# A two-block transformer forward pass on one Trainium2 core: expert weights streamed in pairs of 16 KB rows through ten buffers, with ten units of the fixed expert first

## The reference

```python
def moe_swiglu(u, w_router, w_gate, w_up, w_down):
    logits = (t @ w_router).astype(F32)
    top_vals, top_idx = lax.top_k(logits, TOP_K)
    ...
    for e in range(N_EXPERTS):
        y = swiglu(t, w_gate[e], w_up[e], w_down[e]).astype(F32)
        out = out + gates[:, e:e + 1] * y
```

## Time and profile before

| | us |
|---|---|
| median of 3 runs | 1735.1 (1733.96 to 1736.97) |
| the profiled execution, its own time | 1736.92 |
| its span | 1735.1 |
| mean granted TensorE clock | 0.989 |
| TensorE busy | 1633.8 (94%) |
| VectorE busy | 1000.9 (58%) |
| ScalarE busy | 847.7 (49%) |
| DMA read from HBM | 485.24 MB, 282 GB/s over the span |

### The profile page before, as it was taken

The page is one execution under the profiler, slowest core; times in us unless marked ns, Lnnn a source line. Parts: engine busy times, 40 slices in busy tenths (PEclk is TensorE's granted clock), DMA queues, the critical chain, the costliest instruction groups (busy, mean ns, idle before and its releaser), DMA issues.

```text
span 1735.1 us, 22075 instructions
## 1 busy us (share of the span) xinstructions
PE 1633.8 (94%) x8466; PEld 1178.0 (68%) x8466; DVE 1000.9 (58%) x1347; ACT 847.7 (49%) x1109; POOL 24.2 (1%) x31
## 2 busy tenths in 40 slices
PE   9989899999999999999989999887999989999886
PEld 7877788888878888898766666334665656566432
DVE  7986699847767885577576463004463644645000
ACT  6976677646656553566355353004453544444100
POOL 0000000000000000000000000000000000000000
PEclk9999999999999999999999999999999999999998
DMA  9332355544324555443259999999999999999996
GB/s 377 134 138 97 122 183 183 195 168 170 122 73 176 188 194 194 149 167 134 110 240 422 421 420 419 407 422 414 422 422 421 421 404 422 421 420 422 405 421 272
DMA packets 68940, 490.66 MB, mean 283 GB/s; under 512 B 7776, under 2 KB 8160, under 8 KB 9952
## 3 DMA queue, kind: packets, MB, share of 16 engines
q1 hardware_dynamic: 67248, 484.48, 69.9%
q0 software_dynamic: 1584, 4.72, 1.2%
HBM read 485.24 MB, written 3.93 MB: 282 GB/s over the span
## 4 chain that ended last, share of the span: by engine, by line
PE 68%; DMA 18%; DVE 7%; ACT 5%; issue 1%; POOL 0%; SPq 0%; ACTq 0%; DVEq 0%; POOLq 0%
DMA raw<-in_units 12%; PE ps L495 10%; PE ps L631 9%; PE ps L1408 9%; PE ps L504 8%; PE ps L497 8%; DMA x<-in_units 5%; PE ps L634 5%; PE ps L1425 4%; DVE wl L3533 2%; PE ps L515 2%; DVE wl L2518 1%; ACT wh L2312 1%; PE ps L935 1%; PE ps L936 1%
## 5 line engine op out<-in xcount | busy, mean ns | idle before, releaser
L2518 DVE TENSOR_TENSOR wl<-raw,wh 128x2048 fp32r<-128x2048 f32 x124 | 283.1, 2287 | 81.8 <-ACT wh L1677 81.5
L3533 DVE TENSOR_TENSOR wl<-raw,wh 128x2048 fp32r<-128x2048 f32 x97 | 221.8, 2290 | 171.7 <-ACT wh L2312 171.6
L1677 ACT ACTIVATE wh<-raw 128x2048 fp32r<-128x2048 f32 x125 | 238.4, 1913 | 70.1 <-PE ps L504 69.0
L2312 ACT ACTIVATE wh<-raw 128x2048 fp32r<-128x2048 f32 x96 | 183.7, 1917 | 122.1 <-PE ps L504 121.5
L1408 PE MATMUL ps<-raw,hT_f 128*64 128x512 f32 x424 | 198.0, 612 | 35.0 <-DMA raw<-in_units 33.3
L495 PE MATMUL ps<-wh,hT_both 128*128 128x512 f32 (+2 forms) x568 | 224.4, 397 | 6.3 <-DVE hT_both L2828 1.6
L497 PE MATMUL ps<-wh,hT_both 128*128 128x512 f32 (+2 forms) x568 | 216.8, 384 | 0.0
L1409 PE MATMUL ps<-raw,hT_f 128*64 128x512 f32 x416 | 196.6, 619 | 0.0
L631 PE MATMUL ps<-hT_both,wh 128*128 128x512 f32 x704 | 179.0, 396 | 2.7 <-DVE hT_both L2576 2.6
L1408 PEld LDWEIGHTS ps<-raw,hT_f 128*64 128x64 f32 x424 | 55.7, 140 | 149.4 <-issue 147.8
L504 PE MATMUL ps<-wl,hT_both 128*128 128x512 f32 (+2 forms) x568 | 151.1, 383 | 0.0
(11 more groups left out here) (502 smaller groups left out, 2612.4 us busy)
## 6 DMA issues: line engine op xcount, KB each, us to landing
raw<-in_units SPq DMA_DIRECT2D x384, 1024.0 KB, 14.0
xn<-in_units SPq DMA_DIRECT2D x37, 1024.0 KB, 15.0
x<-in_units SPq DMA_DIRECT2D x37, 1024.0 KB, 15.1
x<-in_x SPq DMA_DIRECT2D x2, 512.0 KB, 5.7
work<-in_lru_w SPq DMA_DIRECT2D x1, 1024.0 KB, 15.9
xn<-in_mem SPq DMA_DIRECT2D x1, 1024.0 KB, 15.4
out<-x POOLq DMA_DIRECT2D x2, 512.0 KB, 3.1
consts<-in_consts POOLq DMA_DIRECT2D x1, 768.0 KB, 4.7
```

The costliest lines, as they stand in the source:

```text
L1677: A(wh[:, n % SPLIT, :], raw[:, n % RAW, :], ACT.Copy).then_inc(sem("hi_made"), 1)
L2312: A(wh[:, (N_FIXED + j) % SPLIT, :], raw_at(n), ACT.Copy).then_inc(sem("hi_made"), 1)
L2518: V.tensor_tensor(wl[:, n % SPLIT, :], raw[:, n % RAW, :], wh[:, n % SPLIT, :].bitcast(F32), ALU.subtract).then_inc(sem("lo_made"), 1)
L3533: V.tensor_tensor(wl[:, s, :], raw_at(STREAM_AT[g, 0, EXPERT_ORDER[j]]), wh[:, s, :].bitcast(F32), ALU.subtract).then_inc(sem("lo_made"), 1)
```

## The change

- The expert weights lie in HBM in pairs: the two halves of a gate, up or down are put side by side, so that one row of a pair has 16 KB. One DMA loads a pair (2 MB) into two neighbouring buffers, and one semaphore tells of both.
- The ring has ten buffers: `raw` gets an eighth, which is also `xn`; the other two are `x` and the last 2048 columns of `work`, side by side. `esg` and the routing tables move out of `work` into `consts`.
- The load of a pair waits until both units of the pair that it overwrites, ten places back, are free.
- The narrow units are loaded in the order gate 0, gate 1, up 0, up 1, where it was gate 0, up 0, gate 1, up 1. TensorE uses them as before.
- `AHEAD = 4` takes the place of `SPLIT` (3) in the stream: four wide units come ahead of the loop. So units 8 to 13 (in the first group 10 to 13) are loaded ahead of the narrow units of chunk 1, and 14 to 19 ahead of those of chunk 2. `SPLIT` is still 3 for `wh` and `wl`.
- In the first group ten units of the fixed expert come first. Seven are loaded as before, the eighth after the last transposes of the stage ahead (`hgrn_oT_ps`), and the ninth and tenth as a pair into the buffers of units 0 and 1, once those are split. All three go ahead of the wait for `ordered`.
- The branch for overfull experts, which is not taken with these inputs, is rewritten for the new layout in HBM.

```diff
-RING = RAW + 2
+RING = RAW + 3
...
-STREAM = [(0, 0, _u) for _u in EXPERT_ORDER[:SPLIT]]
+NARROW_IN_PAIRS = []
+for _c in range(ECH + 1):
+    if _c < ECH:
+        NARROW_IN_PAIRS += [("gate", _c, 0), ("gate", _c, 1), ("up", _c, 0), ("up", _c, 1)]
+    if _c > 0:
+        NARROW_IN_PAIRS += [("down", _c - 1, 0), ("down", _c - 1, 1)]
+AHEAD = 4
+STREAM = [(0, 0, _u) for _u in EXPERT_ORDER[:AHEAD]]
 for _g, (_w, _) in enumerate(GROUPS):
     for _c in range(ECH):
-        _at = 6 * _c + (1 if _c == 0 else -2) + (2 if _c == 0 else 3)
-        _wide = EXPERT_ORDER[_at:_at + (4 if _c == 0 else 6)] if _w is not None else []
-        STREAM += [(_g, 0, _u) for _u in _wide] + [(_g, 1, _u) for _u in NARROW_ORDER if _u[1] == _c - (_u[0] == "down")]
+        _more = 2 if _g == 0 else 0
+        _at = AHEAD if _c == 0 else 2 + 6 * _c + (_more if _c == 1 else 0)
+        _wide = EXPERT_ORDER[_at:_at + (4 + _more if _c == 0 else 6 - _more if _c == 1 else 6)] if _w is not None else []
+        STREAM += [(_g, 0, _u) for _u in _wide] + [(_g, 1, _u) for _u in NARROW_IN_PAIRS if _u[1] == _c - (_u[0] == "down")]
     if _g + 1 < NG and GROUPS[_g + 1][0] is not None:
-        STREAM += [(_g + 1, 0, _u) for _u in EXPERT_ORDER[:SPLIT]]
+        STREAM += [(_g + 1, 0, _u) for _u in EXPERT_ORDER[:AHEAD]]
     STREAM += [(_g, 1, ("down", ECH - 1, _h)) for _h in range(2)]
...
-    x = sb("x", [TT, D])
...
-    xn = sb("xn", [TT, D])
     work_at = nc.sbuf_base
-    work = sb("work", [WORK])
+    work_and_x = sb("work_and_x", [WORK + UNIT])
+    work = work_and_x[:, 0:WORK]
+    x = work_and_x[:, WORK:].rearrange("p (t d) -> p t d", t=TT)
...
+    raw = sb("raw", [RAW + 1, UNIT])
+    xn = raw[:, RAW, :].rearrange("p (t d) -> p t d", t=TT)
...
-    esg = area(11264, HALF)
+    esg = consts[:, dist_at:dist_at + HALF]
...
+    def place_in_ring(n):
+
+        i = n - N_FIXED
+        return i if i <= RAW else (0, 8, 2, 4, 6)[(i - RAW - 1) // 2 % 5] + i % 2
...
+    FIRST_PAIR = N_FIXED + RAW + 1
+
+    def signal_of(n):
+
+        return slot_of(n if n < FIRST_PAIR else n - (n - N_FIXED) % 2)
...
-    spare = [xn_flat, x[:].rearrange("p t d -> p (t d)")]
-
     def raw_at(n):
 
-        return raw[:, slot_of(n), :] if slot_of(n) < RAW else spare[slot_of(n) - RAW]
+        m = place_in_ring(n)
+        at = WORK - UNIT + UNIT * (m - RAW - 1)
+        return raw[:, m, :] if m <= RAW else work_and_x[:, at:at + UNIT]
+
+    def raw_pair(n):
+
+        m = place_in_ring(n)
+        return raw[:, m:m + 2, :].rearrange("p a n -> p (a n)") if m < RAW else work_and_x[:, WORK - UNIT:]
...
+        pairs_d = units_d.rearrange("(a b) p n -> a (b p n)", b=2).rearrange("a (p m) -> a p m", p=P)
+
+        def of_pair(pair, half):
+            return pairs_d[pair][:, half * UNIT:(half + 1) * UNIT]
...
+        for n in range(N_FIXED, N_FIXED + RAW):
+            sp_.wait_ge(sem("lo_made"), n - RAW + 1)
+            load(None, n, of_pair(n // 2, n % 2))
...
+        sp_.wait_ge(*reached("hgrn_oT_ps", 4))
+        n = N_FIXED + RAW
+        sp_.dma_start(raw_at(n), of_pair(n // 2, n % 2)).then_inc(raw_loaded[signal_of(n)], 16)
+        for overwritten in (N_FIXED, N_FIXED + 1):
+            freed(overwritten)
+        sp_.dma_start(raw_pair(FIRST_PAIR), pairs_d[FIRST_PAIR // 2]).then_inc(raw_loaded[signal_of(FIRST_PAIR)], 16)
         sp_.wait_ge(sem("ordered"), 1)
-        at = [nc.sync.value_load(order[0:1, s:s + 1], min_val=N_FIXED, max_val=N_FIXED + (NE - 1) * E_UNITS) for s in range(NE)]
-        for n in range(N_FIXED + RAW, N_UNITS):
+        at = [nc.sync.value_load(order[0:1, s:s + 1], min_val=N_FIXED // 2, max_val=(N_FIXED + (NE - 1) * E_UNITS) // 2) for s in range(NE)]
+        for n in range(FIRST_PAIR + 2, N_UNITS, 2):
             g, narrow, what = STREAM[n - N_FIXED]
-            if n - RING >= N_FIXED:
-                freed(n - RING)
-            elif n == N_FIXED + RAW:
-                sp_.wait_ge(*reached("hgrn_oT_ps", 4))
+            assert what[2] == 0 and STREAM[n + 1 - N_FIXED] == (g, narrow, (what[0], what[1], 1))
+            if n > FIRST_PAIR + 2:
+                for overwritten in (n - RING, n - RING + 1):
+                    freed(overwritten)
             else:
                 sp_.wait_ge(sem("out_written"), 16 * TT)
                 sp_.wait_ge(sem("tokens_left"), 2)
-            sp_.dma_start(raw_at(n), units_d[at[GROUPS[g][narrow]] + UNIT_OF[what]]).then_inc(raw_loaded[slot_of(n)], 16)
+            sp_.dma_start(raw_pair(n), pairs_d[at[GROUPS[g][narrow]] + UNIT_OF[what] // 2]).then_inc(raw_loaded[signal_of(n)], 16)
 
...
-            put(N_FIXED + e * E_UNITS + j, k_tiles(w))
+            beside = [k_tiles(w)] if half == 0 else beside + [k_tiles(w)]
+            if half == 1:
+                put_pair(N_FIXED + e * E_UNITS + j - 1, beside)
```

More of the change, by code:

```diff
@@ L181, in area, with routing_area @@
         return v
+    def routing_area(at, *shape):
+        v = consts[:, CONST["dist"] + at:CONST["dist"] + at + int(np.prod(shape))]
+        return v if len(shape) == 1 else v.rearrange("p (a b) -> p a b", a=shape[0])
     def const(name, n, at=0):
@@ L409, in build @@
     logitsT = work[0:NE, 12992:12992 + S]
[L410 to L417, removed]
+    rcmp = [routing_area(HALF + 128 * i, TT * NE * NE) for i in range(2)]
+    slots = routing_area(768, NE + OVER + 2, TT)
+    places = routing_area(820, NE + OVER, TT)
+    gates = routing_area(868, NE + OVER, TT)
+    by_turn = routing_area(916, NE, NE)
+    place_of, gate_of = routing_area(980, TT, NE), routing_area(996, TT, NE)
+    load_of, turn_of, in_turn_of = routing_area(1012, NE), routing_area(1020, NE), routing_area(1028, NE)
     order = sb("order", [NE], I32)
@@ L451, in fixed_loads @@
         return len(range(slot, N_FIXED, RAW)) if slot < RAW else 1
+    FIRST_PAIR = N_FIXED + RAW + 1
+    def signal_of(n):
+        return slot_of(n if n < FIRST_PAIR else n - (n - N_FIXED) % 2)
     def raw_of(n):
-        return raw_loaded[slot_of(n)], 16 * (fixed_loads(slot_of(n)) + (n - N_FIXED) // RING + 1)
+        slot = signal_of(n)
+        loads = [m for m in range(N_FIXED, n + 1) if signal_of(m) == slot and (m < FIRST_PAIR or (m - N_FIXED) % 2 == 0)]
+        return raw_loaded[slot], 16 * (fixed_loads(slot) + len(loads))
     def raw_again(j):
         slot = (N_FIXED + j) % RAW
-        before = sum(slot_of(n) == slot for n in range(N_FIXED, N_UNITS))
+        before = len([n for n in range(N_FIXED, N_UNITS)
+                      if signal_of(n) == slot and (n < FIRST_PAIR or (n - N_FIXED) % 2 == 0)])
         return raw_loaded[slot], 16 * (fixed_loads(slot) + before + j // RAW + 1)
-    spare = [xn_flat, x[:].rearrange("p t d -> p (t d)")]
     def raw_at(n):
-        return raw[:, slot_of(n), :] if slot_of(n) < RAW else spare[slot_of(n) - RAW]
+        m = place_in_ring(n)
[4 more added lines that the diff above has]
+        return raw[:, m:m + 2, :].rearrange("p a n -> p (a n)") if m < RAW else work_and_x[:, WORK - UNIT:]
     def counted(ins, name, by=1):
@@ L1617, in _ @@
                 sp_.dma_start(rows[:], rows_d.partition_broadcast(P)).then_inc(sem("rows_loaded"), 16)
-        assert (N_FIXED + RAW - head) % RAW == 0 and all(u[:2] == (0, 0) for u in STREAM[:RAW])
-        with nc.sync.Fori(0, (N_FIXED + RAW - head) // RAW) as g:
+        pairs_d = units_d.rearrange("(a b) p n -> a (b p n)", b=2).rearrange("a (p m) -> a p m", p=P)
+        def of_pair(pair, half):
+            return pairs_d[pair][:, half * UNIT:(half + 1) * UNIT]
+        assert (N_FIXED - head) % RAW == 0 and STREAM[:RAW + 3] == [(0, 0, u) for u in EXPERT_ORDER[:RAW + 3]]
+        with nc.sync.Fori(0, (N_FIXED - head) // RAW) as g:
             for j in range(RAW):
@@ L1652, in _ @@
             made_before = N_FIXED + NH * E_UNITS
-            groups = NE * E_UNITS // RAW
-            for j in range(RAW):
-                load(None, N_UNITS + j, units_d[N_FIXED + j])
+            twice = 2 * RAW
+            groups = NE * E_UNITS // twice
+            for j in range(twice):
+                if j < RAW:
+                    load(None, N_UNITS + j, of_pair((N_FIXED + j) // 2, j % 2))
+                else:
+                    again(N_UNITS + j, made_before + j - RAW + 1, of_pair((N_FIXED + j) // 2, j % 2))
             with nc.sync.Fori(1, groups) as g:
-                for j in range(RAW):
-                    again(N_UNITS + j, g * RAW + (made_before + j - RAW + 1), g * RAW + (N_FIXED + j))
+                for j in range(twice):
+                    again(N_UNITS + j, g * twice + (made_before + j - RAW + 1),
+                          of_pair(g * RAW + (N_FIXED + j) // 2, j % 2))
             with nc.sync.Fori(0, groups) as g:
-                for j in range(RAW):
-                    again(N_UNITS + j, g * RAW + (made_before + NE * E_UNITS + j - RAW + 1), g * RAW + (N_FIXED + j))
+                for j in range(twice):
+                    again(N_UNITS + j, g * twice + (made_before + NE * E_UNITS + j - RAW + 1),
```

(5 more changed lines are left out.)

25 lines of the change are left out of this document (13 added, 12 removed).

## The result

Median 1968.4 us of 4 runs (1966.5 to 1970.4), against 1734.5 us for the kernel before, run beside it: ratio 1.1335, 95% interval 1.1321 to 1.1348. The direction and the mechanism were right. The size was not: the profiled execution took 1970.3 us, 233 us more than the one before, where the sum said 193, and the time lies 2 us above the stated range.

A forecast was written before the change was run, and what follows sets the result against it. The prediction took the experts' stage to be bound by its DMA weight stream, TensorE close behind. Three wide groups +196 and narrow-only groups -3.4 gave +193 on 1736.9 (profiled) or 1735.1 (median): 1929 us, range 1892 to 1966.

The forecast's parts named there:

- one period of the locked ring: Wide groups, gate section to gate section: 39.9 us against 29.8, with the clock 41.6, so +11.8 a period.
- the landing of the pairs: After SyncE's issue, the first pair lands in 7.2 us and three more take 14.7 us before the narrow section.
- the clock: Half rate in TensorE's narrow section after each long wait: 1.7 us, between 0 and 3.4.
- The term that decides: Wide groups: unit 13 stays unsplit through the narrow section, holding up later pairs; TensorE idles 12 us; three groups +196.
- The ring suffices: Rival: unit 13 is split in time or the DMA backlog lasts, so only the stream counts: 1716 us; 5%.
- only the order: Rival: only gate, gate, up, up hurts, 3.5 us a wide chunk over 21 chunks: 1789 us; 4%.
- Chunk 6: Sixth chunk of each wide group: only three pairs follow the freed one, so 4.9 us less than a full period: +7.
- Chunk 0 of the three groups: Start of a wide group: the up pair waits for fixed unit 3 and lands at 897.2 us: +2.
- The narrow-only groups: Two groups that stay bound by DMA: 84 units at 0.04 us saved each, -3.4 us.
- The tail stays: End of the run: last down halves arrive together, but their matmuls waited for VectorE (1.02 us), not DMA; no change.
- The early loads earn nothing: Three loads ahead of `ordered`: their 7.5 us of stream only fill the ring that TensorE then has to empty.
- The pairs' packets: Weight stream with 16 KB rows: 4.89 us a pair instead of 4.97, 13 us over 163 pairs if it never stops.

The follow-up runs named there:

- singles: Changed kernel with each half loaded singly, three wide units ahead instead of four: 1740.3 us, against 1868.3 us for the same form with four ahead.
- The mended end: Changed kernel with two units ahead and later splits (1742.6 us), its last chunk's four gate and up units loaded singly in the old order: 1738.1 us.
- The versions without the lock: Changed kernel with pairs kept, two wide units ahead instead of four and later splits: 1742.6 us; variants of it: 1738.1, 1738.0 and 1731.0 us.
- with dummies: Changed kernel with 30 or 16 dummy matmuls into bank 0 in chunks 1 to 6 of each wide group, where TensorE waits: 1948.6 us.

## Why the prediction's mechanism was right, and where its size was wrong

**The step that failed** is the price of one period of the locked ring, and with it the range. The sum had 41.6 us a period, 11.8 more than before; the twelve full periods took 43.0, 13.2 more. Three terms were too low: the landing of the pairs, the start behind it (which had no price) and the clock. The range had room for the clock only. The terms of chunks 0 and 6 and of the end missed to the same side.

**The term that decides held.** Moving the boundary by one or two units took away 189 us (pairs), 128 us (singles), and added 130 us to the kernel before. The first place to look was the right one: which unit of the stream cannot be split, and who stands behind it in SyncE's queue. "The ring suffices" (1716) and "only the order" (1789) are both excluded as accounts of the changed kernel. The granted clock fell once a chunk: it was 0.78 to 0.88 over each of the fifteen narrow sections of chunks 1 to 5. The Trainium skill (TensorE: Matmul & The Clock Gate, HAM oscillation) says that waits for DMA between bursts bring the half rate back at every burst; the trace agrees.

**The terms, measured against the forecast.** The ledger splits the surplus of 40 us (233 for 193):
- Chunks 2 to 5, full periods: +158.2 us in twelve, forecast 141.6; chunk 1, +30.8 in three for 27.4. Together 20 us too little. The issue came as forecast (7.5 us in). A lone pair mostly lands 7.6 to 7.8 us after its issue, not 7.2, and the three that follow are 4.9 apart. With the disturbed periods the fourth lands 22.7 us after the first issue on average, for 21.9; in two of the twelve a packet of the instruction queue fell between, and the first pair took 8.8 to 9.0. TensorE starts 0.14 behind the last; the clock costs 2.2, not 1.7. That is 1.4 us more a period, 17 us over the twelve.
- Chunk 6: +28.9 in three for 21. TensorE waits 7.6 to 7.7 us there, a pair of 4.9 less than the 12.5 of a full period. But I subtracted the 4.9 from a full period's +11.8, from which the slack of 1.4 us that a chunk had before is already taken, and chunk 6 had no slack to lose: it is the chunk with eight wide units. That is 4 of the 8 us.
- Chunk 0 of the three groups: +12.7 for 6. In the first group the up pair lands at 898.2, forecast 897.2, and 1.5 us of half clock follow, which I had charged only from chunk 1 on. In the last wide group the wait in front of the narrow matmuls grew from 1.5 to 5.3 us; why is open.
- The narrow-only groups and the end: +2.8 for -3.4. This step was wrong in kind. "The tail stays" overlooked that the last narrow section needs its gate and up halves 0 only, and that in pairs they are complete one pair later. The mended end shows it: 4.5 us. The first narrow-only group gained nothing either (+0.2 for -1.7), which is left open.

"The early loads earn nothing" is neither confirmed nor excluded: with them behind the router the time was some 4 us longer, within what two runs leave open.

**The range.** Its upper end held the clock at double price and 6 us for the packets, and nothing else. Every small term (0.4 us and more on the landing, 0.14 on the start, 0.5 on the clock) came in on the same side, chunk after chunk; a locked ring passes each of them on to TensorE in full. The rows of before could not show the landing of a lone pair; I had taken the estimate, without a margin.

The pairs' packets were right: the spacing is 4.90 us for a pair against 2 x 2.485 before, 0.07 us saved, an estimated 12 us over the stream's 163 pairs. The versions without the lock show the rate, 427 to 430 GB/s for 421.

## What to carry to other kernels

When loads are issued in one in-order queue into a ring, find the first unit whose buffer cannot come free until a later stage starts, and count who stands behind it; one place in that order was worth 130 us here. Coarser transfers paid here only while a backlog stood; where the queue runs dry, each lone transfer's latency and each extra buffer it waits for comes through in full. Small loads at the start were worth 7 us here, and at the end 4.5. When a split or a copy is moved ahead in an in-order engine, look at what stands behind it.

## What the runs showed of the hardware

- Pairs of 16 KB rows move at 427 to 430 GB/s, 8 KB rows at 421 to 422, in steady stream.
- From issue to landing of a load that nothing stands in front of: 4.6 to 5.2 us for 1 MB, mostly 7.6 to 7.8 us for 2 MB, some 0.4 us more than one landing and one spacing (4.8 + 2.45).
- A 16 KB packet of the instruction queue between issue and landing went with a landing 0.8 to 1.6 us later, in two of twelve periods of the changed kernel and eight of twelve with dummies.
- Waits of 6.7 to 13.8 us in TensorE were followed by 1.5 to 2.9 us lost to the half clock. Dummy matmuls in the wait kept the granted clock at 1.00 in all fifteen narrow sections behind them, and dummies that began after 4.5 idle us ran in part at the half clock themselves (granted 0.82 from 1010 to 1018 us).
